# Sums of squares of q and k by hi and lo halves in fp32r, and the k-products one k-tile later

## What is computed

```python
D_MODEL = 2048; SEQ = 256; GDN_K_HEADS = 16; GDN_V_HEADS = 32; GDN_CHUNK = 64

def l2_normalize(t):
    tf = t.astype(jnp.float32)
    return tf * lax.rsqrt(jnp.sum(tf * tf, axis=-1, keepdims=True) + NORM_EPS)

def gated_deltanet_branch(q, k, v, z, b_logit, a_logit, conv_w, a_log, dt_bias, norm_w):
    qkv = jax.nn.silu(causal_depthwise_conv(jnp.concatenate([q, k, v], axis=-1), conv_w))
    q, k, v = jnp.split(qkv, [GDN_QK_WIDTH, 2 * GDN_QK_WIDTH], axis=-1)
    rep = GDN_V_HEADS // GDN_K_HEADS
    q = jnp.repeat(l2_normalize(q.reshape(bsz, seq, GDN_K_HEADS, GDN_K_DIM)), rep, axis=2)
    k = jnp.repeat(l2_normalize(k.reshape(bsz, seq, GDN_K_HEADS, GDN_K_DIM)), rep, axis=2)
...
    o = chunked_gated_delta_rule(q, k, v, beta, g)
...
def reference(x, c, ...):
        u = x * (1 + scale1) + shift1
        (cb, cc, ch, gq, gk, gv, gz, gb, ga, fq, fk, fv, ff, ma, mb, mc) = jnp.split(
            u @ w_in[l], split_points, axis=-1)
        y_a = short_conv_branch(cb, cc, ch, conv_w[l])
        y_b = gated_deltanet_branch(gq, gk, gv, gz, gb, ga, ...)
        y_c = forgetting_attention_branch(fq, fk, fv, ff, fox_f_bias[l])
        merged = (jax.nn.sigmoid(ma) * (y_a @ w_branch_a[l]) + jax.nn.sigmoid(mb) * (y_b @ w_branch_b[l])
                  + jax.nn.sigmoid(mc) * (y_c @ w_branch_c[l]))
        x = layer_norm(DEEPNORM_ALPHA * x + gate1 * (merged @ w_o[l]), ln1_g[l], ln1_b[l])
        u = x * (1 + scale2) + shift2
        h = jnp.square(jax.nn.relu(u @ w_ff1[l]))
        x = layer_norm(DEEPNORM_ALPHA * x + gate2 * (h @ w_ff2[l]), ln2_g[l], ln2_b[l])
```

## Time and profile before

| | |
|---|---|
| median of 3 runs | 2591.69 us (2587.2 to 2594.75) |
| the profiled execution | 2592.89 us, its span 2591.2 us |
| TensorE busy | 2536.6 us, 98% |
| VectorE, ScalarE busy | 1736.1 us (67%), 1167.1 us (45%) |
| mean granted clock of TensorE | 0.985 |

### The profile page before, as it was taken

The page is one execution under the profiler, slowest core; times in us unless marked ns, Lnnn a source line. Parts: engine busy times, 40 slices in busy tenths (PEclk is TensorE's granted clock), DMA queues, the critical chain, the costliest instruction groups (busy, mean ns, idle before and its releaser), DMA issues.

```text
span 2591.2 us, 33403 instructions
## 1 busy us (share of the span) xinstructions
PE 2536.6 (98%) x12104; PEld 2074.4 (80%) x12104; DVE 1736.1 (67%) x2330; ACT 1167.1 (45%) x1477; POOL 88.2 (3%) x89
## 2 busy tenths in 40 slices
PE   7889999999999999999999999999999999999998
PEld 3567888788888888888888888888888888888886
DVE  4677776787578758776676777766765545546556
ACT  2136354645364355535444444434554444453442
POOL 0001010101001100100000000000000000000000
PEclk8799999999999999999999999999999999999999
DMA  9865657665676567555787877877555665655654
GB/s 308 309 211 166 180 167 227 195 178 164 200 222 179 151 201 239 174 163 164 235 269 249 262 257 247 273 255 248 187 177 189 228 195 189 193 184 194 187 179 141
DMA packets 300463, 540.05 MB, mean 208 GB/s; under 512 B 39184, under 2 KB 44816, under 8 KB 299280
## 3 DMA queue, kind: packets, MB, share of 16 engines
q1 hardware_dynamic: 271040, 522.29, 63.6%
q10 hardware_dynamic: 29264, 15.68, 2.1%
HBM read 534.68 MB, written 3.21 MB: 208 GB/s over the span
## 4 chain that ended last, share of the span: by engine, by line
PE 81%; DVE 7%; ACT 2%; DMA 2%; issue 2%; ACTq 0%; DVEq 0%
PE acc L1807 73%; PE bank L1807 5%; DVE w_lo L1157 3%; PE bank L1810 2%; DMA raw<-in_w_in 2%; ACT w_hi L674 1%; ACT KB L661 1%; DVE W_b L1141 1%; DVE macc L1147 0%; DVE QC L1147 0%; ACTq L874 0%; ACT L661 0%; DMA TT<-inverse_d 0%; DVE W_a L1147 0%; DVE KB L1141 0%
## 5 line engine op out<-in xcount | busy, mean ns | idle before, releaser
L1157 DVE TENSOR_TENSOR w_lo<-raw,w_hi 128x1024 fp32r<-128x1024 f32 x788 | 968.7, 1229 | 587.2 <-ACT w_hi L674 522.7
L674 ACT ACTIVATE w_hi<-raw 128x1024 fp32r<-128x1024 f32 x780 | 814.1, 1059 | 938.6 <-DMA raw<-in_w_in 368.8
L1807 PE MATMUL acc<-w_hi,u_hi 128*128 128x512 f32 x2272 | 905.7, 399 | 11.7 <-DVE w_lo L1157 9.5
L1807 PE MATMUL acc<-w_hi,u_lo 128*128 128x512 f32 x2272 | 890.1, 392 | 0.0
L1807 PE MATMUL acc<-w_lo,u_hi 128*128 128x512 f32 x2272 | 889.5, 392 | 0.0
L1807 PEld LDWEIGHTS acc<-w_hi,u_hi 128*128 128x128 f32 x2272 | 429.5, 189 | 100.9 <-issue 10.7
L1807 PEld LDWEIGHTS acc<-w_hi,u_lo 128*128 128x128 f32 x2272 | 429.3, 189 | 91.4
L1807 PEld LDWEIGHTS acc<-w_lo,u_hi 128*128 128x128 f32 x2272 | 429.9, 189 | 86.1 <-issue 1.0
L1807 PE MATMUL acc<-w_hi,z_hi 128*128 128x512 f32 x880 | 343.7, 391 | 0.0
L1807 PE MATMUL acc<-w_hi,z_lo 128*128 128x512 f32 x880 | 342.6, 389 | 0.0
L1807 PE MATMUL acc<-w_lo,z_hi 128*128 128x512 f32 x880 | 342.4, 389 | 0.0
(11 more groups left out here) (266 smaller groups left out, 1552.7 us busy)
## 6 DMA issues: line engine op xcount, KB each, us to landing
raw<-in_w_in SPq DMA_DIRECT2D x416, 512.0 KB, 4.5
raw<-in_w_ff SPq DMA_DIRECT2D x256, 512.0 KB, 4.5
raw<-in_w_ada SPq DMA_DIRECT2D x192, 512.0 KB, 4.7
raw<-in_w_branch_a SPq DMA_DIRECT2D x32, 512.0 KB, 5.1
raw<-in_w_branch_b SPq DMA_DIRECT2D x32, 512.0 KB, 5.2
raw<-in_w_branch_c SPq DMA_DIRECT2D x32, 512.0 KB, 5.2
raw<-in_w_o SPq DMA_DIRECT2D x32, 512.0 KB, 5.3
IT<-decay_d ACTq DMA_DIRECT2D x8, 512.0 KB, 7.0
```

The costliest lines, as they stand in the source:

```text
L674: a.activation(weights(n)[0], raw[:, rl % RAWS, :, :], ACT.Copy).then_inc(hi_ready.sem, 1)
L1157: v.tensor_tensor(lo, raw[:, rl % RAWS, :, :] if src is None else src, hi, ALU.subtract).then_inc(lo_ready.sem, 1)
L1807: return t_.matmul(dst, lhsT, rhs, start=start, stop=stop)
```

## The change

Squares are no longer summed in fp32. ScalarE copies each square to fp32r (`sq_hi`, in the memory of `TT`), VectorE subtracts it from the square (`sq_lo`, over the square itself), and TensorE multiplies both with an fp32r `ones_r` into one bank. The squares stay at position 42 (now `AT_SQ`), the sums go from k-tile 46 to 47, ScalarE's Ln from 47 to 48, and the k-products from 56 and 59 to 57 and 60, with VectorE's `low` one position on as well.

```diff
--- before.py
+++ after.py
@@ -103,7 +103,7 @@
 
 MOD_BANK = (0, 3)
 
-AT_LAST, AT_SSQ, AT_GV, AT_KK, AT_LOW = 2, 46, 52, (56, 59), 62
+AT_LAST, AT_SQ, AT_SSQ, AT_GV, AT_KK, AT_LOW = 2, 42, 47, 52, (57, 60), 62
 AT_TOK, AT_BLOCKS, AT_MOD0, AT_INVERSE, AT_FQ = 67, 67, 70, 75, 82
 AT_W, AT_D = (86, 91), (88, 93)
 AT_Y, AT_Z, AT_X, AT_O = (95, 102), (96, 103), (98, 105), (99, 106)
@@ -319,6 +319,7 @@
         cur_cwg = sb("cur_cwg", [P, 3, TAPS_G, BPC])
         cur_cwa = sb("cur_cwa", [P, TAPS_A, BPC])
         eps_b = sb("eps_b", [P, 3])
+        ones_r = sb("ones_r", [P, P], F32R)
         fmax = sb("fmax", [P, 2, MT * KPC])
         rms = sb("rms", [P, MT * VPC])
         macc = sb("macc", [P, 2, NC])
@@ -331,6 +332,8 @@
         BI = sb("BI", [P, KPC, 3 * P], at=at0 + 4 * KPC * 3 * P)
         PT = sb("PT", [P, KPC, 3 * P], at=at0 + 8 * KPC * 3 * P)
         osq = [TT[:, 2 + m, :, :].rearrange("p a b -> p (a b)") for m in range(MT)]
+        sq_lo = sb("sq_lo", [P, 4, NC], F32R, at=at0)
+        sq_hi = sb("sq_hi", [P, 4, NC], F32R, at=at0 + 2 * 4 * KPC * QH * P)
         norm_tmp = [KB[:, n, :, :].rearrange("p a b -> p (a b)") for n in range(4)]
 
         x_sb = sb("x_sb", [P, MT, D], at=y_at)
@@ -411,7 +414,7 @@
                 beta_made=1, beta_turned=1, sums_done=1, sums_in=1, decay_left=1, heads_made=1, ln_var=1, ln_root=1, half_done=1, out_made=1,
 
                 macc_ready=MODS, mcol_done=MODS, mod_made=MODS,
-                turned=3, taps_in=1, tap_made=3, conv_made=3, silu_made=3, sq_made=1, ssq_done=1, rn_made=1, qk_made=1,
+                turned=3, taps_in=1, tap_made=3, conv_made=3, silu_made=3, sq_hi_made=4, sq_lo_made=4, ssq_done=1, ones_cast=1, rn_made=1, qk_made=1,
                 tok_done=2, k_tok_in=1, v_tok_in=1,
                 d_made=4, decay_made=4, kk_done=4, low_made=4, it_masked=4, tt_zero=1, yn_zero=1,
                 inv_made=1, t_turned=2 * len(LEVELS), w_done=4 * len(LEVELS), w_made=4 * len(LEVELS),
@@ -731,6 +734,8 @@
                 activate(uT[:, 2 * n:2 * n + 2, :].rearrange("p a b -> p (a b)"), bank[2 + n % 2][:, :], ACT.Copy, "x_copied", n + 1)
             act.wait_ge(g_in.sem, 16 * 4)
             activate(gpar[:, 0:VH], gpar[:, 0:VH], ACT.Exp)
+            act.wait_ge(N["masks_made"].sem, 1)
+            activate(ones_r[:, :], ones[:, :], ACT.Copy, "ones_cast", 1)
             o.after()
 
             row_copy(1)
@@ -829,13 +834,16 @@
                     o.after()
                     act.dma_start(beta_d[:, :, :].rearrange("m h c -> h m c"), beta_T[0:VH, :, :]).then_inc(beta_out.sem, 16)
                     act.dma_start(decay_d[:, :, :].rearrange("m h c -> h m c"), decay_T[0:VH, :, :]).then_inc(decay_out.sem, 16)
-                to(AT_SSQ - 4)
+                to(AT_SQ)
                 silu(0, QC)
                 silu(1, KC)
                 o.after()
                 for n in range(4):
                     src = (QC, KC)[n // 2][:, 2 * (n % 2):2 * (n % 2) + 2, :]
-                    activate(norm_tmp[n], src.rearrange("p a b -> p (a b)"), ACT.Square, *(("sq_made", 1) if n == 3 else ()))
+                    activate(norm_tmp[n], src.rearrange("p a b -> p (a b)"), ACT.Square)
+                o.after()
+                for n in range(4):
+                    activate(sq_hi[:, n, :], norm_tmp[n], ACT.Copy, "sq_hi_made", n + 1)
                 if i == 0:
                     act.wait_ge(decay_out.sem, 16)
                     load_decay()
@@ -1406,6 +1414,13 @@
                     taps((QC, KC, VC)[k], halves(2 * (k % 2)), lambda b, tap: cur_cwg[:, k, tap, b:b + 1], TAPS_G, "conv_made", k + 1,
                          between, 1)
 
+                def square_lows():
+
+                    to(AT_SSQ)
+                    for n in range(4):
+                        wait("sq_hi_made", n + 1)
+                        tt(sq_lo[:, n, :], norm_tmp[n], sq_hi[:, n, :], ALU.subtract, "sq_lo_made", n + 1)
+
                 if i == 0:
                     to(AT_SMALL)
                     small_start()
@@ -1418,6 +1433,7 @@
                 if i == 0:
                     to(AT_SUMS + 2)
                     small_sums()
+                    square_lows()
                     to(AT_DECAY)
                     take_heads()
                 dve.wait_ge(decay_in.sem, decay_in.value(i, 16 * MT))
@@ -1427,6 +1443,8 @@
                         t, r = divmod(q, 2)
                         ts(IT[:, h, q, :], IT[:, h, q, :], cur[:, 0, t, 2 * h + r:2 * h + r + 1],
                            0.0, ALU.subtract, ALU.min, *(("d_made", h + 1) if q == QH - 1 else ()))
+                if i:
+                    square_lows()
                 to(AT_GV)
                 wait("rn_made", 1)
                 for n in range(4):
@@ -2021,12 +2039,15 @@
                     small_sums()
                 to(AT_SSQ)
 
-                wait("sq_made", 1)
+                if i == 0:
+                    wait("ones_cast", 1)
                 wait("conv_made", 2)
                 if i == 0:
                     pe.wait_ge(N["decay_left"].sem, 1)
                 for n in range(4):
-                    last = mm(bank[n][:, :], ones[:, :], norm_tmp[n])
+                    wait("sq_lo_made", n + 1)
+                    mm(bank[n][:, :], ones_r[:, :], sq_hi[:, n, :], True, False)
+                    last = mm(bank[n][:, :], ones_r[:, :], sq_lo[:, n, :], False, True)
                 last.then_inc(N["ssq_done"].sem, 1)
                 to(AT_GV)
                 wait_taken(i, J_GV)
```

## The result

| | before | after |
|---|---|---|
| median, 5 runs each | 2591.7 us | 2609.7 us |
| range of the runs | 2587.2 to 2594.75 | 2605.9 to 2613.3 |
| profiled execution, its span | 2592.9, 2591.2 | 2609.9, 2608.2 |

What follows compares the result with a forecast made beforehand. TensorE, busy for 98% of the span, was taken as the bound. Terms 20.7 + 2.0 + 2.0 - 6.7 - 3.6 - 0.2 + 1.2 = +15.4 us, +21 with the clock, gave a 2613 us median, range 2602 to 2624.

Steps and rivals of the forecast that it cites:

- E+6.9: First sq_lo ready 6.9 us after E, the end of ScalarE's squares, behind copies, two w_hi, w_lo and first subtraction.
- Stalls 20.7: TensorE's waits for the first sq_lo at k-tile 47, summed over four blocks: +20.7 us.
- The clock: Granted clock falls to half after the sq_lo stall in each block: +1.6 us per block, +6.4 in all.
- -6.7 + 2.0 + 2.0 + 6.4 = +3.7: Four-block terms: fp32r products -6.7, sq_lo pairs 0.6 apart +2.0, wait for gv's stage +2.0, half clock +6.4.
- the 5.2 us: Assumed length of half clock after each stall's restart, the mean of 6.0, 5.7, 5.5 and 3.5 us.
- The rival in which the clock holds: Granted clock stays full behind the stalls: +15 us, 2607 us; chance 0.12.
- the one with 10 us: Half clock lasts 10 us after each stall: +4 us per block above full clock, 2623 us; chance 0.12.
- The rival without the rate: ones_r products come 0.43 us apart like the fp32 ones, so 6.7 us are not saved: 2620 us; chance 0.05.
- The wait for gv's stage: At k-tile 52 TensorE waits 0.5 us per block for ScalarE's chain at full clock, +2.0 us.
- 1.2 less 0.8: Lateness at the turned V, k-tile 67: +1.2 us at full clock, less 0.8 covered by half clock in three blocks.
- The -3.6: TensorE's 4.3 us of waits for scaled KC at the k-products go, except 0.7 in block 0: -3.6 us.
- the 10.5 us of savings: TensorE's savings without stalls: fp32r products 6.7, KC waits 3.6, old wait on squares 0.2; rival at 2581 us, chance 0.04.

Runs made afterwards that it cites:

- lows_first: The changed kernel with VectorE's four subtractions no longer held to position 47, so ahead of the w_lo of tiles 43 and 45; 2593.1 us, ratio 1.0025 to the kernel before.
- hi_only: The changed kernel without the lo halves: no subtractions, TensorE sums sq_hi alone by four fp32r products; 2597.7 us against 2589.4 for the kernel before, ratio 1.0037.
- filler: The changed kernel with twenty 512-column matmuls of unread result ahead of the wait for sq_lo; 2603.6 us, ratio 1.0061 to the kernel before.
- kk56: scale_early with block 0's subtractions in a row before the scaling, low one position earlier, k-products back at 56 and 59; 2580.9 us against 2590.0, ratio 0.9966.
- the positions alone: The kernel before, fp32 sums kept, with sums moved to k-tile 47 and k-products to 57 and 60; 2588.1 us against 2588.7, ratio 0.9999.
- q_first: The changed kernel with queues rearranged: q's squares and copies at position 37 in blocks 1 to 3, earlier subtractions, stage between Ln and Exp; 2589.8 us against 2589.4.
- scale_early: q_first with VectorE's scaling of QC and KC moved to position 49 (block 0: behind the first four subtractions); 2587.7 us, ratio 0.9991 to the kernel before.

## Why the prediction was right

The forecast was 2613 us, 21 above the profiled execution; the median after is 2609.7, 18 above the median before, and from block 0 on the profiled execution cost 22.0. The wait that decides came where and as long as the sum has it; that the other terms add up as well is in part luck, as the last points say.

- **The queue** ahead of the first `sq_lo` came as added up: E+6.9 forecast, E+6.9 measured in block 1. Stalls 20.7 forecast, 21.0 measured; by block 4.45, 5.7, 5.3, 5.3 against 5.01, 6.06, 4.48, 5.40. The queue was as exact in the other blocks: first product at E+6.87 and E+6.86 in the blocks 2 and 3, and at E+8.49 in block 0, where 8.45 was forecast. All the misses by block come from where TensorE stood when the squares ended: it reached k-tile 47 at E+3.48, 0.80, 2.39 and 1.46, where 4.01, 1.2, 1.6 and 1.6 were taken. That these cancel in the sum is luck. lows_first shows that the order makes the wait: same work, 4.8 us of it. What the sum did not see is that this stall covered a second one, ScalarE's, which hi_only laid open.
- **The clock** was the mis-sized term. It fell in all four blocks, but TensorE's steps behind the wait were 0.43 only until 215.5, 495.6, 775.5 and 1055.4, that is for 4.4, 3.6, 3.3 and 4.4 us, where 5.2 were assumed. In three blocks it had begun to fall within the wait (0.79, 0.74 and 0.79 in the blocks 0, 1 and 3), which costs nothing, and most of the half rate then lay on the eight products, which would have waited for `sq_lo` anyway. From the first product to the turn of gv's stage the four blocks took 10.90, 10.87, 10.75 and 10.87 us; before, less one k-tile of 1.36, 10.29, 10.41, 10.30 and 10.29. That is +2.1 in all for products, pairs, clock and stage, where -6.7 + 2.0 + 2.0 + 6.4 = +3.7 was forecast. At full clock the sum was right: by it the stretch takes 9.6 us, and filler has 9.65, 9.67 and 9.65, with the pairs 0.6 apart as forecast. So the clock cost 1.2 us per block and not 1.6.
- **Where the 5.2 us came from.** They were the mean of four stretches behind waits in the first 150 us, and those do not show what such a wait does to a full clock: it stood at 0.50 already while TensorE waited, in all four. That they came near is luck. The last row below is the stretch behind the 2.0 us wait in the kernel before, of which the earlier trace rows has only the wait itself.

```profile
50.20:52.30 2.10, 0.00 (x0) 0.50 0.78 211
81.00:83.30 2.30, 0.09 (x1) 0.50 1.05 390
112.00:114.30 2.30, 0.00 (x0) 0.50 1.05 387
141.50:143.60 2.10, 0.00 (x1) 0.50 0.00 0
...
230.40:234.40 4.00, 3.98 (x26) 1.00 0.40 119
```

- The rival in which the clock holds is out; the one with 10 us too. Of what the Trainium skill says in 'TensorE: Matmul & The Clock Gate', 'HAM oscillation — how this bites in real kernels' (the price is paid again at every recurrence), the trace agrees: half clock in four blocks of four.
- **fp32r rate.** After, it cannot be seen, since the products ran at half clock, 0.43 apart. Where nothing is waited for they stand 0.23 apart (kk56 above), as the row of the main products said, and not at the 131 ns that the Trainium skill gives in 'TensorE: Matmul & The Clock Gate', 'Back-to-back issue gap'. The rival without the rate is out.
- **The wait for gv's stage** was forecast at 0.5 per block with the clock full and at nothing with it down. It was 0.27 and 0.29 in the blocks 1 and 2, where half clock ended soonest; at full clock filler has 0.29 to 0.32 in three blocks and the positions alone 0.30 in all four. The mechanism holds, at 0.3 and not 0.5. For V, 1.2 less 0.8 was forecast, 0.4; it waited 0.84, in one block.
- **KC**: forecast 0.7 left in block 0, measured 0.66 there and nothing elsewhere. The -3.6 was entered as a gain, with +1.2 given back at V. The positions alone showed no gain (0.9999), so what was given back, at V and at later waits for `stage`, is nearer to the whole of it; this step was too kind to the change.
- The terms do not close exactly: 21.0 - 0.2 + 2.1 - 3.6 + 0.8 and 0.7 for later waits make 20.8 of the 22.0. So 1.6 too much at the clock were made up by V, by the later waits and by 1.2 us that no term has, and that the total came within 1 us is luck in this part. The 1.2 seem to lie in block 0: from its first k-products to where TensorE reached the sums of block 1 it took 255.45 us (230.50 to 485.95) against 253.97 before (230.42 to 484.39), the same number of k-tiles and no wait in the list; the reason stays open.

My own theory of the experiments, that open queues would let the 10.5 us of savings through, fell twice (q_first, scale_early). Each time the wait moved on along one chain (sums, stage, scaled KC, low, V), whose next member stood behind w_hi or w_lo in some queue.

## What to carry to other kernels

Cost a new step by what is queued ahead of it on the engine that makes it, up to the instruction that waits: here 1.7 us less of matmuls per block were bought with 5.2 us of queue. Where one wait is long, ask what it hides on the other engines, because taking it away shows the next one, and often only moving a whole chain forward gains time. Moving a waiting consumer one step later removes its wait on the list and also starts everything behind it later; the median, not the list, says whether it paid.

## What was not expected of the hardware

A wait of 2.01 us left the granted clock at 1.00 (230.40:234.40 above); in the kernel with the filler one of 2.00 was followed by 0.50 for 3.4 us, and in lows_first two of 1.94 by 1.00. After a wait of 3.85 us (hi_only) 0.50 stood for the next 3 us, of 3.54 (scale_early) 0.59 for 3.2. So waits of like length differ in what they cost, and the length alone does not tell it. In three of four blocks of the change the clock fell within the wait, in block 2 only behind it (1.00 during its 4.5 us), without the next stretch being longer.
